# A two-block network in one kernel: first-tile memory attention moved into the row gathers, input weights asked for before a stage boundary, longer filler

## The reference

```
x    = rmsnorm(h, g_final)                       # end of block one
proj = x @ w_in_a                                # 1024 -> 768 + 768 + 256
u, gv = gelu(proj[:, :768]), layer_norm(gelu(proj[:, 768:1536]))
qm   = proj[:, 1536:]                            # 4 heads of 64
mix  = u * (causal w_s @ gv + b_s)               # per group of 64 columns
mo   = softmax(qm @ mk.T / 8) @ mv               # 256 memory rows, keys and values from mem
x    = layer_norm(ALPHA * x + concat(mix, mo) @ w_out)
expert, gate = route(x)                          # top 2 of 16
x    = layer_norm(ALPHA * x + moe_ffn(x, expert, gate))
```

## Time and profile before

| | |
|---|---|
| median of 3 timed runs | 2173.28 us (2166.62 to 2174.05) |
| the profiled execution's own time | 2165.67 us |
| its span, first to last instruction | 2164.0 us |
| busy: TensorE products, VectorE, ScalarE, GpSimd | 83%, 37%, 19%, 14% |
| mean granted TensorE clock | 0.929 of full |
| moved by DMA | 761.41 MB, 352 GB/s over the span |

### The profile page before, as it was taken

The page is one execution under the profiler, slowest core; times in us unless marked ns, Lnnn a source line. Parts: engine busy times, 40 slices in busy tenths (PEclk is TensorE's granted clock), DMA queues, the critical chain, the costliest instruction groups (busy, mean ns, idle before and its releaser), DMA issues. The chain is left out here.

```text
span 2164.0 us, 23134 instructions
## 1 busy us (share of the span) xinstructions
PE 1795.7 (83%) x9272; PEld 902.4 (42%) x9272; DVE 804.1 (37%) x1916; ACT 417.8 (19%) x978; POOL 298.7 (14%) x286
## 2 busy tenths in 40 slices
PE   9999997786665555657999998888799999988886
PEld 7576883453331111114453333333268533333332
DVE  3746146676667777764230111010123401100102
ACT  2272113222111212223211000000124200000001
POOL 1000013454344443440000000000000000000000
PEclk9999998898887876679999999999989999999999
DMA  7224529999999999996669999999952899999997
GB/s 254 79 115 178 214 99 397 405 397 422 421 421 422 421 421 421 421 421 262 263 254 428 427 426 427 427 427 426 425 224 94 349 426 426 427 427 426 427 428 300
DMA packets 78570, 761.41 MB, mean 352 GB/s; under 512 B 8638, under 2 KB 9441, under 8 KB 17266
## 3 DMA queue, kind: packets, MB, share of 16 engines
q1 hardware_dynamic: 40818, 489.47, 54.2%
q0 software_dynamic: 37632, 270.32, 30.4%
HBM read 758.71 MB, written 1.05 MB: 351 GB/s over the span
## 5 line engine op out<-in xcount | busy, mean ns | idle before, releaser
L2411 PE MATMUL bank<-arena 128*64 128x512 f32 x3072 | 677.7, 595 | 72.2 <-DMA arena<-in_w_up 46.2
L874 PE MATMUL bank<-arena 64*64 64x512 f32 x2032 | 327.3, 799 | 240.9 <-ACT arena L609 236.8
L2411 PEld LDWEIGHTS bank<-arena 128*64 128x64 f32 x3072 | 213.4, 137 | 523.7 <-issue 394.6
L411 POOL DMA_INDIRECT arena<-in_peer_uv,arena x256 | 286.1, 1118 | 673.8 <-PE bank L874 306.8
L1167 DVE CUSTOM_DVE_ANT_0 arena<-arena 128x1024 f32<-128x1024 f32 x256 | 313.9, 1226 | 175.0 <-DMA arena<-in_peer_uv,arena 163.8
L874 PEld LDWEIGHTS bank<-arena 64*64 64x64 f32 x2032 | 94.1, 180 | 458.6 <-ACT arena L609 268.1
L2523 DVE TENSOR_TENSOR arena<-arena,bank 128x512 f32<-128x512 f32 x32 | 22.0, 688 | 680.9 <-PE bank L2411 680.9
L650 PE MATMUL bank<-arena 128*128 128x272 f32 (+2 forms) x768 | 145.4, 349 | 0.5 <-ACT arena L443 0.3
L650 PEld LDWEIGHTS bank<-arena 128*128 128x128 f32 x768 | 126.2, 191 | 20.4 <-issue 3.2
L604 ACT ACTIVATE arena<-arena 128x4 f32<-128x4 f32 (+1 forms) x65 | 13.3, 205 | 472.8 <-DVE arena L1167 472.7
L1243 POOL DMA_DIRECT2D arena<-in_w_router x2 | 1.1, 572 | 582.4 <-POOLq L2301 552.5
(11 more groups left out here) (414 smaller groups left out, 1559.0 us busy)
## 6 DMA issues: line engine op xcount, KB each, us to landing
arena<-in_w_up SPq DMA_DIRECT2D x64, 2048.0 KB, 38.3
arena<-in_w_gate SPq DMA_DIRECT2D x64, 2048.0 KB, 39.3
arena<-in_w_down SPq DMA_DIRECT2D x64, 2048.0 KB, 40.8
arena<-in_w_in SPq DMA_DIRECT2D x14, 2048.0 KB, 9.9
arena<-in_w_out SPq DMA_DIRECT2D x2, 4096.0 KB, 21.0
arena<-in_wq SPq DMA_DIRECT2D x4, 2048.0 KB, 14.0
arena<-in_rg_out SPq DMA_DIRECT2D x1, 4096.0 KB, 16.8
arena<-in_peer_uv,arena POOLq DMA_INDIRECT x256
```

What stands on the lines that cost most here:

```text
L411: nc.gpsimd.indirect_dma_start(SLOT[slot_of[j]], None, d["peer_uv"], bass.IndirectOffsetOnAxis(IDX[:, u % 4, k:k + 1], 0)).then_inc(s_row[ ...
L874: m = pe.matmul(bank[banks[t][half]][to:to + HALF, :], DIAG[lo:lo + HALF, k + j, :], row[lo:lo + HALF, D + half * 512:D + (half + 1) * 512 ...
L2411: x = pe.matmul(bank[b][j * C:(j + 1) * C, :], operand[:, c, j * C:(j + 1) * C], RING[s % AHEAD][:, c % (DC // 2), j, :], start=(c == 0), ...
```

## The change

A class `MemoryHeads` holds one token tile's memory attention as steps per engine. For tile 0 the steps are issued in the front stage, in groups 56 to 62, and for tile 1 in the gating stage. Tile 0's output and norm move from groups 56 to 61 to groups 52 to 56. The 2 MB part `a` of the input weights is asked for when the last picked row has landed, and tile 0's product with it (job (a, 0)) is done at the end of the front stage; `b` and `c` are asked for when tile 1's norm is done. ScalarE loads the Gelu table before the boundary. In the gating stage jobs `q` and (a, 0) are gone; the output product is issued in quarters, and the load of the Sqrt table comes behind the last transposed chunk. The filler in both routers grows from 24 to 36 products, and that at the start of both expert stages from 4 to 8.

```diff
+class MemoryHeads:
...
+    def tensor_turn(self, pe):
+        K, t = self.K, self.tile
+        for n in range(2):
+            for c in range(4):
+                m = pe.transpose(K.bank[self.turn_banks[n]][:, c * P:(c + 1) * P], K.h_res[:, t, (4 * n + c) * P:(4 * n + c + 1) * P], K.ident)
+            m.then_inc(self.s_mm, 1)
+
+    def scalar_turned(self, act, a):
+        for n in range(2):
+            act.wait_ge(self.s_mm, HX_TURNED + n + 1)
+            a.activation(self.XT[:, 4 * n:4 * n + 4, :], self.K.bank[self.turn_banks[n]][:, :].rearrange("p (a b) -> p a b", a=4),
+                         ACT.Copy).then_inc(self.s_act, 1)
+
+    def tensor_queries(self, te, pe):
+        K = self.K
+        te.wait_ge(K.s_win_q, 16)
+        te.wait_ge(self.s_act, HX_COPIED + 2)
+        for i in range(MEM_PAIRS):
+            for c in range(DC):
+                m = pe.matmul(K.bank[self.query_bank][:, i * P:(i + 1) * P], K.WIN_Q[:, c, i * P:(i + 1) * P], self.XT[:, c, :],
+                              start=(c == 0), stop=(c == DC - 1))
+        m.then_inc(self.s_mm, 1)
+
+    def scalar_queries(self, act, a):
+        act.wait_ge(self.s_mm, HQ_MM)
+        a.activation(self.QT, self.K.bank[self.query_bank][:, 0:MEM_PAIRS * P].rearrange("p (a b) -> p a b", a=MEM_PAIRS),
+                     ACT.Copy).then_inc(self.s_act, 1)
+
+    def tensor_scores(self, te, pe):
+        K = self.K
+        te.wait_ge(self.s_act, HQ_COPIED)
+        for p in range(MEM_PAIRS):
+            for j in range(2):
+                r = slice(j * HD, (j + 1) * HD)
+                m = pe.matmul(K.bank[self.score_banks[j]][:, p * T:(p + 1) * T], self.QT[r, p, :], K.MKT[0][r, p, :], start=True, stop=True)
+                if p == MEM_PAIRS - 1:
+                    m.then_inc(self.s_mm, 1)
+
+    def vector_scores(self, ve, do, v):
+        K = self.K
+        do(v.memset(self.LSUM_ALL, 0.0))
+        for j in range(2):
+            ve.wait_ge(self.s_mm, HS_MM + j + 1)
+            do(v.tensor_scalar(self.SB[:, j, :, :], K.bank[self.score_banks[j]][:, :].rearrange("p (a k) -> p a k", a=MEM_PAIRS),
+                               ATT_SCALE, None, ALU.mult))
+            v.tensor_reduce(self.NEGM[:, :, j], self.SB[:, j, :, :], X_AXIS, ALU.max, negate=True).then_inc(self.s_vec, 1)
+
+    def scalar_exps(self, act, a):
+        for j in range(2):
+            act.wait_ge(self.s_vec, H_MAX + j + 1)
+            for p in range(MEM_PAIRS):
+                a.activation(self.SB[:, j, p, :], self.SB[:, j, p, :], ACT.Exp, bias=self.NEGM[:, p, j:j + 1],
+                             accum_out=self.LSUM[:, p, j:j + 1]).then_inc(self.s_act, 1)
+
+    def tensor_p_turned(self, te, pe):
+        K = self.K
+        for j in range(2):
+            te.wait_ge(self.s_act, H_EXPS + MEM_PAIRS * (j + 1))
+            for p in range(MEM_PAIRS):
+                for k in range(2):
+                    n = 2 * p + k
+                    m = pe.transpose(K.bank[self.p_banks[j]][:, n * P:(n + 1) * P], self.SB[:, j, p, k * P:(k + 1) * P], K.ident)
+            m.then_inc(self.s_mm, 1)
+
+    def scalar_p_turned(self, act, a):
+        for j in range(2):
+            act.wait_ge(self.s_mm, HP_TURNED + j + 1)
+            a.activation(self.PT[:, j, :, :], self.K.bank[self.p_banks[j]][:, :].rearrange("p (a b) -> p a b", a=2 * MEM_PAIRS),
+                         ACT.Copy).then_inc(self.s_act, 1)
+
+    def tensor_values(self, te, pe):
+        K = self.K
+        for j in range(2):
+            te.wait_ge(self.s_act, HP_COPIED + j + 1)
+            for p in range(MEM_PAIRS):
+                cols = slice((2 * p + j) * HD, (2 * p + j + 1) * HD)
+                for k in range(2):
+                    m = pe.matmul(K.bank[self.value_bank][:, cols], self.PT[:, j, 2 * p + k, :], K.MV[0][:, k, cols],
+                                  start=(k == 0), stop=(k == 1))
+        m.then_inc(self.s_mm, 1)
+
+    def vector_values(self, ve, do, v):
+        ve.wait_ge(self.s_act, HP_COPIED)
+        do(v.reciprocal(self.RL_ALL, self.LSUM_ALL))
+        ve.wait_ge(self.s_mm, HV_MM)
+        v.tensor_tensor(self.out.rearrange("p (h e) -> p h e", h=MEM_H),
+                        self.K.bank[self.value_bank][:, 0:MEM_W].rearrange("p (h e) -> p h e", h=MEM_H),
+                        self.RL_ALL.unsqueeze(2).to_broadcast([P, MEM_H, HD]), ALU.mult).then_inc(self.s_vec, 1)
...
+    TILE_0_OUT = (UNITS - 3) * QUADS
+    HEADS_FROM = (UNITS - 2) * QUADS
...
+            sp.wait_ge(s_idx, UNITS)
+            sp.wait_ge(s_xf, TT)
+            sp.wait_ge(s_row[slot_of[-1]], landed[-1])
+            sp.dma_start(WINA, d["w_in0"].rearrange("(c p) n -> p c n", p=P)[:, :, 512:1024]).then_inc(s_win_a, 16)
+            sp.wait_ge(s_xf, TT + TT)
+            for n, at, lo in (("b", WIN_B, 1024), ("c", WIN_C, 0)):
+                sp.dma_start(cut(at, P, DC, 512), d["w_in0"].rearrange("(c p) n -> p c n", p=P)[:, :, lo:lo + 512]).then_inc(K.s_win[n], 16)
...
-                    if u == UNITS - 2 and q == 2:
+                    if n == TILE_0_OUT + 2:
                         final_squares(0)
-                    if u == UNITS - 2 and q == 3:
+                    if n == TILE_0_OUT + 3:
                         final_root(0)
+                    if n == HEADS_FROM + 1:
+                        heads.scalar_turned(act, a)
+                    if n == HEADS_FROM + 2:
+                        heads.scalar_queries(act, a)
+                    if n == HEADS_FROM + 4:
+                        heads.scalar_exps(act, a)
+                    if n == HEADS_FROM + 5:
+                        heads.scalar_p_turned(act, a)
             a.activation(WARM, ONE, ACT.Sqrt)
             final_squares(1)
             final_root(1)
+            a.activation(WARM, ONE, ACT.Gelu)
...
+                        if n == HEADS_FROM:
+                            te.wait_ge(s_xf, TT + 1)
+                            heads.tensor_turn(pe)
+                        if n == HEADS_FROM + 1:
+                            heads.tensor_queries(te, pe)
+                        if n == HEADS_FROM + 2:
+                            heads.tensor_scores(te, pe)
+                        if n == HEADS_FROM + 4:
+                            heads.tensor_p_turned(te, pe)
+                        if n == HEADS_FROM + 5:
+                            heads.tensor_values(te, pe)
+            te.wait_ge(s_win_a, 16)
+            for c in range(DC):
+                m = pe.matmul(bank[A0_BANK][:, :], heads.XT[:, c, :], WINA[:, c, :], start=(c == 0), stop=(c == DC - 1))
+            m.then_inc(K.s_a0, 1)
...
-                    if u == UNITS - 2 and q < 2:
-                        add_crossed(0, q)
-                        add_straight(0, q)
-                    if u == UNITS - 2 and q == 3:
+                    if n in (TILE_0_OUT, TILE_0_OUT + 1):
+                        add_crossed(0, n - TILE_0_OUT)
+                        add_straight(0, n - TILE_0_OUT)
+                    if n == TILE_0_OUT + 3:
                         final_mean(0)
-                    if u == UNITS - 1 and q == 1:
+                    if n == TILE_0_OUT + 4:
                         final_norm(0)
+                    if n == HEADS_FROM + 3:
+                        heads.vector_scores(ve, do, v)
+                    if n == HEADS_FROM + 6:
+                        heads.vector_values(ve, do, v)
...
-        keep_busy(pe, K.bank[self.idle_bank], K.ident, 24)
+        keep_busy(pe, K.bank[self.idle_bank], K.ident, 36)
...
-    JOBS = [("q", 0), ("q", 1), ("a", 0), ("b", 0), ("a", 1), ("b", 1), ("c", 0), ("c", 1)]
+    JOBS = [("a", 0), ("b", 0), ("a", 1), ("b", 1), ("c", 0), ("c", 1)]
+    JOB_BANKS = (A0_BANK, 1, 0, 1, 0, 1)
...
+            sp.wait_ge(heads.s_mm, HQ_MM)
...
-            sp.wait_ge(s_pm, len(JOBS))
+            sp.wait_ge(s_pm, len(JOBS) - 1)
...
+            heads.scalar_turned(act, a)
             leave("a", 0)
-            for h in range(MEM_H):
-                act.wait_ge(s_tm, h + 1)
-                a.activation(PT[:, h, :, :], bank[TURNED[h // 2][h % 2]][:, :].rearrange("p (a b) -> p a b", a=4),
-                             ACT.Copy).then_inc(s_pt, 1)
+            heads.scalar_queries(act, a)
             leave("b", 0)
+            heads.scalar_exps(act, a)
             leave("a", 1)
-            act.wait_ge(s_tm, MEM_H)
+            heads.scalar_p_turned(act, a)
...
             mix_turned(0)
             leave("c", 1)
+            for n in range(1, 4):
+                mix_turned(n)
             act.wait_ge(s_zero, 2)
             a.activation(WARM, WARM, ACT.Sqrt)
-            for n in range(1, 4):
-                mix_turned(n)
...
+            heads.tensor_queries(te, pe)
+            project("b", 0)
+            heads.tensor_scores(te, pe)
             router.tensor_weights(te, pe, bank[7])
-            project("a", 0)
-            turn(0)
-            turn(1)
-            project("b", 0)
-            te.wait_ge(s_sc, MEM_H)
-            values(0)
```

(20 more changed lines are left out.)

183 lines of the change are left out of this document (68 added, 115 removed).

## The result

The changed kernel takes 2148.98 us in the median of five runs (2147.48 to 2152.72), the kernel before beside it 2171.04 (2164.66 to 2174.05). The ratio is 0.9913, with a 95% interval of 0.9902 to 0.9924: 18.9 us off 2171.04, where 16.3 had been forecast. The profiled execution took 2147.93 us, its span is 2146.2 against 2164.0, 17.8 less.

A forecast was written before the change was run, and what follows sets the result against it. TensorE's own work ahead of the first expert product was taken as the bound; 9.1 + 4.8 + 1.4 + 1.0 = 16.3 us off the median 2173.28 gave 2157.0, range 2147 to 2168.

The forecast's parts named there:

- A microsecond at the first expert product is one at the end: Expert stage: TensorE reaching its first expert product a microsecond earlier takes a microsecond off the kernel's end.
- The boundary: Front to gating stage: `a` lands after 8.2 us, product (a, 0) follows, gating stage starts at 1009.0, 7.0 us later.
- the 1.7 us charged for the clock behind 2.1 us of idling: Boundary: TensorE idles 2.1 us before product (a, 0), the clock falls and the product takes 1.7 us more.
- The first rival: Boundary: `a` lands after 7.1 us or less and the clock holds; 19.1 us off, 2154.2; chance 0.17.
- Gating stage to the gate products: Gating stage: 37.4 us from TensorE's start to the gate products, which begin 9.1 us earlier than before.
- the second chain: Gating stage: values, then VectorE's gate mean and norm, end 37.1 us from the start, level with TensorE.
- Behind the gates: From the end of (c, 1) to the router: output product in quarters, without waits or low clock, gains 4.8 us.
- The fillers: Routers and expert stages: longer fillers keep the clock whole in the packing, gaining 1.4 us in the first stage, 1.0 in the second.
- the second rival: Clock falls everywhere it can: fillers lose 4.2 us, the load lands late; 8.5 us off, 2164.8; chance 0.16.
- The gathers: Front stage: tile 0's attention work fits the groups' free time, covered by the row queue; cost 0, without cover up to 16.8 us.
- the slower rival: Front stage: gather stream runs dry, three inserted waits cost 10 us each; 13.7 us slower, 2187; chance 0.04.

The follow-up runs named there:

- e5: Changed kernel with product (a, 0) also waiting for VectorE's last norm of the second tile, so TensorE idles longer; 2153.95 us, ratio 0.9941.
- e12: Changed kernel with TensorE's transposes and products of tile 1's memory attention issued twice in the gating stage; 2156.22 us, ratio 0.9945.
- e4: Changed kernel with loads `a`, `b`, `c` asked for at the gating stage's start and product (a, 0) done there, tile 0's attention left early; 2156.23 us, ratio 0.9945.
- e8: Changed kernel with the loads of `b` and `c` asked for at the gating stage's start; 2155.03 us, ratio 0.9941.
- e3: Changed kernel with the output product in halves again and the Sqrt table load ahead of the later copies; 2152.87 us, ratio 0.9938.
- e7: Kernel before with only the output product in quarters and the Sqrt load behind the fourth copy; 2160.30 us, ratio 0.9968.
- e6: Kernel before with only the longer fillers, 36 in the routers and 8 ahead of the packing; 2166.11 us, ratio 0.9990.
- e1: Changed kernel with the fillers of before, 24 in the routers and 4 in the expert stages; 2150.16 us, ratio 0.9918.
- e2: Changed kernel with 30 filler products in the routers instead of 36, and 8 in the expert stages; 2149.87 us, ratio 0.9920.
- e11: Changed kernel with 36 fillers in the routers and 4 instead of 8 ahead of the packing; 2148.93 us, ratio 0.9905.
- e9_again: The changed kernel run and profiled once more with no edit; 2147.94 us, ratio 0.9899.

## Why the prediction was right, and where it was off

The forecast was 2157.0, the median 2148.98. Of the 8.0 us between them 2.2 are the level, since before's median here was 2171.04 and not 2173.28. The other 5.8 are the difference of the medians, 22.1, against the 16.3 that stood; of these the ratio bears out 2.6 (18.9) and the spans 1.5 (17.8), the rest is scatter of the medians. That the spans come within 1.5 us is in part luck. Beyond the forecast they hold 2.4 us at the boundary and in the gating stage, 0.5 behind it, and 2.15 of scatter in the first expert stage; against it stand 2.5 of a later last row, 0.6 less from the fillers and 0.6 at the end.

- **A microsecond at the first expert product is one at the end.** Right. In all fourteen profiles the first expert product is followed by the second router after 565.2 to 567.4 us. The 2.15 us that the changed kernel gained there lie inside that spread; they are no part of the change.
- **The boundary.** Forecast: load of `a` 8.2 us, measured 7.8; stage start 1009.0, measured 1009.30 though the last row came 2.47 later. The mis-sized step is the 1.7 us charged for the clock behind 2.1 us of idling: TensorE idled 1.70 and lost nothing, nor did it in the eight other profiles that idled 1.49 to 1.76 there, and behind 3.90 (e5) it lost 1.67. The Trainium skill (DMA: Bandwidth & Descriptors, "Anatomy of one DMA") would have the load land after 6.8 us, an estimate by its formula, which is fitted for loads of GpSimd; the ten profiles that start it alone, from SyncE, have 7.6 to 7.9. The first rival was right on the clock and not on the load.
- **Gating stage to the gate products.** Forecast 37.4, measured 37.16, with the second chain 0.3 us below TensorE, where 37.1 had been said. e12 shows that TensorE sets it. From the last sums on the two steps together gave 11.55 us, 2.4 more than the forecast 9.1: 1.7 the clock, 0.4 the load, 0.2 the stage.
- **Joined.** With the attention early and all three loads late (e4) that distance is 56.14; with the loads early and TensorE's attention work put back (e12) it is 1052.93 - 995.02 = 57.91. So against before's 61.52 the one gives 5.4 us, the other 3.6, both together 11.6. Either alone leaves something the other removes: in e4 the idling, the clock and the wait for `a`. Asking early for `a` alone is not enough: with `b` and `c` late (e8) the distance is 56.83, 4.7 less than before.
- **Behind the gates.** Forecast 4.8, measured 5.2 and reproduced both ways up to the router (e3, e7). Up to the first expert product it is another number. The 4.8 and the 5.2 hold about 1.7 us for a fall of the clock behind the idle time; without the idle time the clock mostly fell behind the product instead. Beside e3, with the same fillers, the changed kernel gains 3.6 us up to there (56.04 and 52.43); in the kernel before, with 24 and 4, quarters take the distance from 1123.53 - 1065.63 = 57.90 us to 1118.29 - 1066.68 = 51.61 (e7), 6.3 less. The forecast counted the clock as won here and gave no chance to a fall further on in place of this one.
- **The fillers.** Forecast 1.4 and 1.0, measured 0.2 and 1.6 in the one profile. The step that failed is that a filler which fills the gap keeps the clock: it kept it in the packing, as said, but the clock fell in the router's filler itself. At 36 and 8 a stage takes 22.0 us where the clock stays whole, 23.7 where it falls, and 25.3 where it stays down twice as long; the mean over eight profiles is 23.5, and over three profiles at 24 and 4 it is 22.9. One fall in each stage (e8, 23.66 twice) still left the two stages 0.2 us shorter than before's, not 4.2 longer as the second rival had it. e6 and e1 cannot be told from no effect. As far as these runs show, the longer filler is worth nothing.
- **The gathers.** Forecast 0. The share stays at 1.01, so the stream did not run dry. Of the last row's 2.47 us, 1.9 stand at the 208th of the 256 dot products, the last before group 52, with which the moved work begins; over that stretch profiles of the same code differ by more (559.38 us in e1, 556.04 in e5, 556.73 in before). From the 208th dot product to the last it is 121.0 to 121.2 us in the eleven profiles with the moved work (121.16 in the changed kernel's) and 120.4 to 120.6 in the three without (120.58 in before's). So the moved work costs 0.6 us, and the rest is the execution's; the 10 us of the slower rival are ruled out.

Two things stay open. Why the clock falls in a busy TensorE at the router in some executions wasn't found: it does so behind transposes and products of 16 columns. With quarters it fell somewhere between (c, 1) and the first expert product in all profiles but e2 and e11, and each of these is a single one. And tile 0's attention was not put back into the gating stage as it was, with its work on ScalarE and VectorE; e12 gives TensorE's share alone. None of the versions beats the changed kernel beyond the error of its time.

## What to carry to other kernels

Work moved over a stage boundary pays in full where the engine's timeline behind it has no gaps, but only if its operands are asked for early too: attention without the early loads gave 5.4 us, the early loads with TensorE's share of the attention put back 3.6, both 11.6. Look for table loads and copies that a long product could cover before moving anything larger: ordering the output product by what is ready gave 5.2 us up to the router with no data moved. Follow such a gain to the next common mark, since a lower clock that an idle time had brought can come back behind it: here 3.6 of the 5.2 were left at the first expert product. A filler should be judged over several profiles, since one profile of it can be off by 1.6 or 3.2 us.

## What the hardware showed that was not expected

The granted clock fell to its lower level with no idle time in front: 0.57 from 1090 to 1094 us in the changed kernel, in the middle of products that ran back to back, and in e9_again in the 16-column products themselves. A fall cost 1.6 us, or 3.2 where the clock stayed down twice as long, and the same kernel had one short fall in these two stretches in one execution and a short and a long one in the other: 9.81 and 8.29 us for its two fillers, then 9.91 and 10.67. The Trainium skill (TensorE: Matmul & The Clock Gate, "What's actually happening") says of a kernel's start that the number of products at the lower clock differs from run to run of the same kernel; these two profiles show such a difference in the middle of one.

A 2 MB load landed after 7.6 to 7.9 us alone, after 8.1 with a second one behind it, and after 10.6 with that, more loads of SyncE and three small ones of GpSimd behind it (e8). All these were issued after it, so later loads can delay an earlier one by 2.5 us; which of them did was not tested.
